# Prompt attention with keys on partitions and rounded products, in a one-core encoder layer

## What is computed

```python
q = (cq @ lp['w_uq']).reshape(B, S, N_HEADS, QK_NOPE + QK_ROPE)
qn, qr = q[..., :QK_NOPE], rope(q[..., QK_NOPE:], pos)
kv = (lat @ lp['w_ukv']).reshape(B, lat.shape[1], N_HEADS, QK_NOPE + V_HEAD)
kn, v = kv[..., :QK_NOPE], kv[..., QK_NOPE:]
sc = mla_scores(qn_b, qr_b, kn, kr)          # 96 features, scaled by 96 ** -0.5
sc = jnp.where(key_chunk[None, :] <= q_chunk[:, None], sc, -jnp.inf)
p = jax.nn.softmax(sc, axis=-1).astype(v.dtype)
return jnp.einsum('bhqk,bkhd->bqhd', p, v)
```

## Time and profile before

| | |
|---|---|
| median of three runs | 1743.34 us |
| profiled execution, its own time | 1737.2 us |
| its span | 1735.4 us |
| mean granted TensorE clock | 0.976 of 2.4 GHz |
| TensorE, VectorE, ScalarE, GpSimd busy | 93%, 57%, 43%, 14% |
| prompt attention, first turned queries to last scaled rows | 323.9 to 525.5 us |
| chain that ended last, TensorE's share | 58% |

### The profile page before, as it was taken

One profiled execution on the slowest core, in us unless ns is written; L12 is line 12 of the kernel. 1 busy time (PEld: TensorE's weight loads), 2 busy tenths in 40 slices (PEclk: granted clock), 3 DMA queues, 4 the chain that ended last, 5 costly groups with the idle time before them and its releaser, 6 DMA issues.

```text
span 1735.4 us, 21728 instructions
## 1 busy us (share of the span) xinstructions
PE 1612.0 (93%) x8282; PEld 1292.7 (74%) x8282; DVE 993.6 (57%) x1347; ACT 751.8 (43%) x1062; POOL 249.4 (14%) x210
## 2 busy tenths in 40 slices
PE   8999999799998899999999998999999999999966
PEld 4578877466766688999877777788888888888852
DVE  1410111366665456422344447889988889889936
ACT  2311111332335202222332113588778778788834
POOL 0000000000007173000021110111111121111104
PEclk9999999999999999999999897999999999999988
DMA  9510111700002354300054445799999999999967
GB/s 356 216 62 29 61 53 47 240 20 20 10 12 98 146 192 172 134 25 13 22 184 149 143 136 216 258 376 379 379 383 387 376 389 385 390 383 377 363 231 299
DMA packets 134295, 351.77 MB, mean 203 GB/s; under 512 B 24498, under 2 KB 27186, under 8 KB 128708
## 3 DMA queue, kind: packets, MB, share of 16 engines
q1 hardware_dynamic: 124084, 330.69, 51.6%
q0 software_dynamic: 9216, 18.89, 2.8%
q10 hardware_dynamic: 912, 1.05, 0.2%
HBM read 322.19 MB, written 43.15 MB: 211 GB/s over the span
## 4 chain that ended last, share of the span: by engine, by line
PE 58%; DMA 20%; DVE 13%; ACT 4%; issue 3%; SPq 1%; POOL 0%; DVEq 0%; POOLq 0%; ACTq 0%
DMA beside<-in_w_exp_up 18%; PE M L911 11%; DVE rounded L1629 10%; PE T L753 6%; PE M L744 5%; PE M L816 3%; PE T L689 3%; PE M L1159 3%; PE T L806 3%; PE M L689 2%; PE T L970 2%; ACT rounded L1517 2%; PE T L972 2%; PE T L971 2%; PE M L999 2%
## 5 line engine op out<-in xcount | busy, mean ns | idle before, releaser
L1159 PE MATMUL M<-rounded 128*128 128x512 f32 x2304 | 548.9, 395 | 11.2 <-DVE conv_w_rows L1960 5.6
L1629 DVE TENSOR_TENSOR rounded<-beside,rounded 128x1024 fp32r<-128x1024 f32 (+2 forms) x394 | 468.0, 1234 | 114.3 <-ACT rounded L1517 56.6
L1159 PEld LDWEIGHTS M<-rounded 128*128 128x128 f32 x2304 | 429.1, 189 | 105.6 <-issue 15.0
L1517 ACT CAST rounded<-beside 128x1024 fp32r<-128x1024 f32 x256 | 259.2, 1050 | 94.9 <-DMA beside<-in_w_exp_up 88.1
L911 PE MATMUL M<-rounded 128*128 128x512 f32 x864 | 216.5, 407 | 5.2 <-DVE logits L1852 2.3
L911 PEld LDWEIGHTS M<-rounded 128*128 128x128 f32 x864 | 164.9, 195 | 43.6 <-issue 7.9
L1527 ACT CAST rounded<-beside 128x1024 fp32r<-128x1024 f32 x128 | 125.3, 1048 | 19.5 <-DMA beside<-in_w_exp_down 17.2
L2201 POOL DMA_INDIRECT expert_rows<-beside,route_out x32 | 44.4, 1389 | 380.1 <-ACT beside L1558 360.6
L1341 ACT ACTIVATE arena<-T,negmax 128x384 f32<-128x384 f32 (+3 forms) x64 | 47.4, 740 | 114.6 <-DVE negmax L1706 114.6
L1629 DVE TENSOR_TENSOR rounded<-T,rounded 128x512 fp32r<-128x512 f32 (+1 forms) x82 | 81.7, 1000 | 26.2 <-ACT rounded L1401 18.2
L689 PE MATMUL T<-tables,arena 128*128 128x128 f32 x572 | 77.8, 284 | 17.3 <-DMA arena<-in_mem_prompt 6.7
(11 more groups left out here) (302 smaller groups left out, 2107.5 us busy)
## 6 DMA issues: line engine op xcount, KB each, us to landing
beside<-in_w_exp_gate SPq DMA_DIRECT2D x64, 1024.0 KB, 8.5
beside<-in_w_exp_up SPq DMA_DIRECT2D x64, 1024.0 KB, 11.3
beside<-in_w_exp_down SPq DMA_DIRECT2D x32, 2048.0 KB, 11.6
arena<-x_rows SPq DMA_DIRECT2D x27, 512.0 KB, 4.0
x_rows<-arena SPq DMA_DIRECT2D x18, 512.0 KB, 3.0
arena<-expert_rows SPq DMA_DIRECT2D x9, 1024.0 KB, 12.8
arena<-in_x_prompt SPq DMA_DIRECT2D x16, 512.0 KB, 3.9
arena<-in_cache_mem_k SPq DMA_DIRECT2D x8, 1024.0 KB, 5.8
```

The source lines that it names most:

```text
L1159: got = nc.tensor.matmul(out, x[xs], (high, low)[ws](w)[:, c:c + 512], start=(first and n == 0), stop=(last and n == 2))
L1517: nc.scalar.copy(high(c), w_raw[c // 4][:, c % 4, :]).then_inc(gu_high, 1)
L1629: return nc.vector.tensor_tensor(out, x, highs.bitcast(f32), ALU.subtract)
```

## The change

Prompt attention is turned: keys stand on partitions, queries along the columns. For each key tile j (0 to 7) `scores` makes the scores of all queries from tile j on, up to 1024 columns, as three rounded products; the masked corners are left out of the exponential and are zeros set once in `p_hi` and `p_lo`. A softmax needs each query's maximum before that. So a first, single rounded product (`lead_scores`, 12 pieces of up to 512 columns in M[0]) gives scores with queries on partitions, VectorE takes their negated maxima (`largest`), and the maximum is written as a 97th feature beside the 96 of each query (`qh[..][:, i, HW:AUG]`), against a row of ones under the keys. The queries are turned again with it (`turn_with_max`), scaled, and split in high and low. ScalarE takes the exponential twice (`exponentials`), to `p_raw` and rounded to `p_hi`; GpSimd subtracts them to `p_lo`. `weigh_values` multiplies 64 value columns beside 64 columns of ones (`v_high`, `v_low`, which stay put) with them, three products, so that M[1] collects result and row sum for each query along the columns; `divide_rows` takes the reciprocal of 64 x 512 sums and multiplies, per half of a head, into `attnT`. The result already has the form in which mixing wants it, so `turn_mix` turns only the conv rows; `conv_rows` has three buffers instead of four.

In the loop over n = 8h + j, TensorE issues scores of n, values of n-2, and for head h+1 lead products (`STEPS`), the second turn, then for head h+2 queries and keys. VectorE's order is keys of h+1, maxima 0 to 2, second half of head h-1's division, maxima 3 to 11, first half of head h's division, low halves of the scaled queries of h+1. w_ukv is loaded after the memory's stores; heads 0 and 1 are loaded before the last tile's stores; w_out's chunks 0 to 3 are loaded after the stage, behind two sets of conv rows.

The core of the diff (of the replaced loops on each engine, which are printed above, only the new side stands here):

```diff
-    ORDER = (2, 4, 6, 7, 5, 3, 1, 0)
+    LEADS = [(i, c, min(c + 512, (i + 1) * 128)) for i in (7, 6, 5, 4, 3, 2, 1, 0) for c in range(0, (i + 1) * 128, 512)]
...
-        conv_rows = [area(at, CW) for at in (46848, 47360, 45312, 45824)]
+        conv_rows = [area(at, CW) for at in (46848, 47360, 45824)]
...
-            sp.wait_ge(mem_ps, 8)
-            sp.dma_start(w_ukv, A["w_ukv"].rearrange("l p (h c) -> p (l h) c", h=H)).then_inc(win_lo_in, 16)
+            sp.wait_ge(mem_out, 48)
+            sp.dma_start(w_ukv, A["w_ukv"].rearrange("l p (h c) -> p (l h) c", h=H)).then_inc(win_lo_in, 16)
...
+            def load_head(h):
+                u = h % 2
+                sp.dma_start(qh[u][:, :, 0:HW], q_heads[:, :, h * HW:(h + 1) * HW]).then_inc(head_in[u], 16)
+                sp.dma_start(wk[u], w_ukv_cols[:, h * (DN + DV):h * (DN + DV) + DN]).then_inc(head_in[u], 16)
+            for u in (0, 1):
+                sp.wait_ge(q_out[u], 16 + 16 * 4)
+            sp.wait_ge(xT_ps, NT)
+            load_head(0)
+            load_head(1)
             store_rows(LAST_TILE)
...
+            sp.dma_start(lat_all, cache_lat).then_inc(cache_in[0], 16)
+            for k in range(4, KT):
                 sp.dma_start(w_out_raw[k], w_out_rows[:, k, :]).then_inc(win_lo_in, 16)
-            sp.dma_start(q_s, q_dram[PT * P:, :].rearrange("p (h c) -> p h c", h=H)).then_inc(sq_in, 16)
-            sp.dma_start(lat_all, cache_lat).then_inc(cache_in[0], 16)
-            sp.dma_start(lat_new[0:ROWS, :, :], lat_s.rearrange("(b r) c -> r b c", r=ROWS)).then_inc(sq_in, 16)
...
-            for t in range(4):
+            load_conv(0)
+            load_conv(1)
+            for k in range(4):
+                sp.dma_start(w_out_raw[k], w_out_rows[:, k, :]).then_inc(win_lo_in, 16)
+            for t in (2, 3):
                 load_conv(t)
...
+            def turn_queries(h):
+                u = h % 2
+                pe.wait_ge(head_in[u], 32 * (h // 2) + 32)
+                for half in (0, 1):
+                    if h > 0:
+                        pe.wait_ge(qa_ready, 2 * (h - 1) + half + 1)
+                    for i in range(4 * half, 4 * half + 4):
+                        got = nc.tensor.transpose(M[0][0:HW, i * P:(i + 1) * P], qh[u][:, i, 0:HW], ident)
+                    got.then_inc(qT_ps, 1)
+            def keys(h):
+                for half in (0, 1):
+                    pe.wait_ge(qT_ready, 2 * h + half + 1)
+                    cols = slice(half * 512, half * 512 + 512)
+                    nc.tensor.matmul(M[0][0:DN, cols], wk[h % 2], latT[:, cols], start=True, stop=True).then_inc(kT_ps, 1)
+            def lead_scores(h, c):
+                i, c0, c1 = LEADS[c]
+                if c < 2:
+                    pe.wait_ge(kT_ready, 2 * h + c + 1)
+                else:
+                    pe.wait_ge(negmax_ready, MAXES * h + c - 1)
+                at = (c % 2) * 512
+                nc.tensor.matmul(M[0][:, at:at + c1 - c0], q_lead[0:HW, i * P:(i + 1) * P], kT_hi[h % 2][0:HW, c0:c1],
+                                 start=True, stop=True).then_inc(lead_ps, 1)
+            def turn_with_max(h):
+                for half in (0, 1):
+                    pe.wait_ge(negmax_ready, MAXES * h + len(LEADS) + half)
+                    for i in range(4 * half, 4 * half + 4):
+                        got = nc.tensor.transpose(M[0][0:AUG, i * P:(i + 1) * P], qh[h % 2][:, i, 0:AUG], ident)
+                    got.then_inc(pT_ps, 1)
+            def by_banks(j):
+                return [(max(c, j * P), c + 512) for c in (0, 512) if j * P < c + 512]
+            def scores(n):
+                h, j = divmod(n, PT)
+                u = h % 2
+                if n > 1:
+                    pe.wait_ge(exp_done, n - 1)
+                if j == 0:
+                    pe.wait_ge(qa_ready, 2 * h + 2)
+                for c0, c1 in by_banks(j):
+                    for m, (k, q) in enumerate(((kT_hi, qa_hi), (kT_hi, qa_lo), (kT_lo, qa_hi))):
+                        got = nc.tensor.matmul(T[n % 2][:, c0:c1], k[u][0:AUG, j * P:(j + 1) * P], q[u][0:AUG, c0:c1],
+                                               start=(m == 0), stop=(m == 2))
+                got.then_inc(s_ps, 1)
+            def weigh_values(n):
+                h, j = divmod(n, PT)
+                at = (h % 2) * DV
+                pe.wait_ge(p_ready, n + 1)
+                if j == 0 and h > 0:
+                    pe.wait_ge(o_done, 2 * h)
+                for c0, c1 in by_banks(j):
+                    for m, (v, p) in enumerate(((v_high, p_hi), (v_high, p_lo), (v_low, p_hi))):
+                        got = nc.tensor.matmul(M[1][:, c0:c1], v[:, j, h // 2, at:at + 2 * DV], p[n % 3][:, c0 - j * P:c1 - j * P],
+                                               start=(j == 0 and m == 0), stop=(m == 2 and j == c1 // P - 1))
+                got.then_inc(o_ps, 1)
...
+            turn_with_max(0)
+            turn_queries(1)
+            keys(1)
+            pe.wait_ge(value_ready, PT)
+            pe.wait_ge(pads_zero, 2)
+            STEPS = ((0, 1, 2), (3, 4, 5), (6, 7), (8, 9), (10, 11))
+            for n in range(PT * H):
+                h, j = divmod(n, PT)
+                scores(n)
+                if n > 1:
+                    weigh_values(n - 2)
+                if h + 1 < H:
+                    if j < 5:
+                        for c in STEPS[j]:
+                            lead_scores(h + 1, c)
+                    if j == 5:
+                        turn_with_max(h + 1)
+                if h + 2 < H:
+                    if j == 6:
+                        turn_queries(h + 2)
+                    if j == 7:
+                        keys(h + 2)
+            weigh_values(PT * H - 2)
+            weigh_values(PT * H - 1)
...
-                if t < PT:
-                    transposes(T[u], attn[:, t, :], 4)
-                transposes(T[u][:, 512:], conv_rows[t % 4], 4).then_inc(rowsT_ps, 1)
+                transposes(T[u][:, 512:], conv_rows[t % 3], 4).then_inc(rowsT_ps, 1)
...
+            def queries_high(h):
+                for half in (0, 1):
+                    cols = slice(half * 512, half * 512 + 512)
+                    act.wait_ge(qT_ps, 2 * h + half + 1)
+                    nc.scalar.copy(q_lead[0:HW, cols], M[0][0:HW, cols]).then_inc(qT_ready, 1)
+            def keys_high(h):
+                for half in (0, 1):
+                    cols = slice(half * 512, half * 512 + 512)
+                    act.wait_ge(kT_ps, 2 * h + half + 1)
+                    if h > 1:
+                        act.wait_ge(s_ps, PT * (h - 1))
+                    nc.scalar.copy(kT_hi[h % 2][0:DN, cols], M[0][0:DN, cols]).then_inc(kT_high, 1)
+            def scaled_high(h):
+                for half in (0, 1):
+                    cols = slice(half * 512, half * 512 + 512)
+                    act.wait_ge(pT_ps, 2 * h + half + 1)
+                    nc.scalar.mul(qa_hi[h % 2][0:AUG, cols], M[0][0:AUG, cols], MLA_SCALE).then_inc(qa_high, 1)
+            def exponentials(n):
+                j = n % PT
+                act.wait_ge(s_ps, n + 1)
+                if n > 1:
+                    act.wait_ge(p_ready, n - 1)
+                if n > 2:
+                    act.wait_ge(o_ps, n - 2)
+                nc.scalar.activation(p_raw[n % 2][:, 0:D - j * P], T[n % 2][:, j * P:], ACT.Exp)
+                nc.scalar.activation(p_hi[n % 3][0:64, 0:64], T[n % 2][0:64, j * P:j * P + 64], ACT.Exp)
+                nc.scalar.activation(p_hi[n % 3][:, 64:D - j * P], T[n % 2][:, j * P + 64:], ACT.Exp).then_inc(exp_done, 1)
...
+            for n in range(PT * H):
+                h, j = divmod(n, PT)
+                exponentials(n)
+                if j == 5 and h + 1 < H:
+                    scaled_high(h + 1)
+                if j == 6 and h + 2 < H:
+                    queries_high(h + 2)
+                if j == 7 and h + 2 < H:
+                    keys_high(h + 2)
...
+            def keys_low(h):
+                for half in (0, 1):
+                    cols = slice(half * 512, half * 512 + 512)
+                    dve.wait_ge(kT_high, 2 * h + half + 1)
+                    take_low(kT_lo[h % 2][0:DN, cols], M[0][0:DN, cols], kT_hi[h % 2][0:DN, cols]).then_inc(kT_ready, 1)
+            def largest(h, c):
+                i, c0, c1 = LEADS[c]
+                at = (c % 2) * 512
+                end = at + c1 - c0
+                dve.wait_ge(lead_ps, len(LEADS) * h + c + 1)
+                if c1 == (i + 1) * P:
+                    nc.vector.memset(M[0][0:64, end - 64:end], FAR).then_inc(dve_step, step.next())
                     dve.wait_ge(dve_step, step.value())
+                into = qh[h % 2][:, i, HW:AUG] if i < 4 else part_max[:, i - 4, c0 // 512:c0 // 512 + 1]
+                nc.vector.tensor_reduce(into, M[0][:, at:end], AX.X, ALU.max, negate=True).then_inc(negmax_ready, 1)
+            def larger_part(h):
```

(39 more changed lines are left out.)

342 lines of the change are left out of this document (154 added, 188 removed).

## The result

The changed kernel takes **1829.1 us** (median of four runs, 1826.5 to 1835.8) against 1741.3 before: a ratio of 1.051, interval 1.0471 to 1.0548. It is slower, as forecast, but by 88 us where 54 were forecast, and 9 above the range. The profiled execution was the slowest of the four, 1835.8 with a span of 1834.0; the other three spans were 1824.6 to 1827.3.

The account below looks back on a forecast made before the run. TensorE, in prompt attention, was taken to bound the kernel. Later cache start 40.2, weights +3.1, mixing -4.1 and clock +14.5 sum to 53.7 us on the median 1743.3: 1797 us, range 1769 to 1820.

Parts of the forecast that it names:

- the mechanism: Prompt attention: each head's two VectorE divisions stand ahead of something TensorE needs; period 29.8 us, 4.8 more than before.
- the two pauses: TensorE idle in each head before the sixth lead product (5.4 us) and before the next queries' transposes (3.7 us).
- The reciprocal: VectorE's reciprocal of 64 x 512 sums takes 4.1 us, from the 1 and 9 column rows; bounds 1.5 and 4.5.
- TensorE's work: Products, transposes and keys of one head in prompt attention sum to 19.3 us against 25.0 before.
- the clock: After the stage's pauses TensorE returns at a granted clock of 0.50, 1.2 GHz; together +14.5 us.
- Pause B: TensorE waits before the next queries' transposes for the first half's division and scaled low half: idle 3.7 us, clock +4.5.
- A: TensorE's lead 5 waits for maximum 3, behind the previous head's division: idle 5.4 us, seven times, clock +10.0.
- Rival 3: Slower still: both pauses leave TensorE at 1.2 GHz for longer, 68 us more in all, 1812; chance 0.2.
- The start: Edge before the first head: maxima end at 338.0, second head's queries and keys take 4 us, scores begin at 342.0.
- three tiles ahead, which is enough: Mixing: a third conv buffer instead of a fourth leaves GpSimd three tiles ahead, taken as enough, at no cost.
- The fallback price: Mixing: if GpSimd's cover were gone, a late conv tile would cost about 9 us, once.
- The weights: Cache part: w_out chunks land 12 us after the stage, and ScalarE's first cache exponential waits for them: +3.1 us.

Follow-up runs that it names:

- experiment 2: The changed kernel with two VectorE steps exchanged, the low half of the scaled queries before the division of a head's first half: 1792.4 us (1.0326).
- experiment 4: The changed kernel with every reciprocal of 64x512 issued twice: 1884.7 us (1.0838).
- experiment 7: The changed kernel with ScalarE copying values and sums out of the accumulator, and VectorE dividing once per pair of heads and half: 1757.1 us (1.011).
- the filled pauses: The changed kernel with 16 and 11 products that nothing reads put into a head's two pauses: 1799.3 us (1.0349).
- experiment 9: The changed kernel with paired divisions, convolutions in the old order, earlier loads, and products that nothing reads at the stage's two edges: 1730.0 us (0.9936).
- experiment 1: The changed kernel with GpSimd's old convolution order in mixing (convolution t+4 behind deviation t), still three buffers: 1810.9 us (1.0429).
- experiment 5: The changed kernel with convolution rows and four w_out chunks issued after the last product instead of the last division: 1829.7 us (1.0524).

## Why the prediction was right and wrong

**Right: the mechanism.** Both divisions lie on TensorE's way, ahead of a maximum and of the low half of the queries; the two pauses appear there, idle 4.4 and 3.1 us. Experiments 2, 4 and 7 show it from three sides: exchange the order, double the cost, take it away. That ScalarE and GpSimd hide beside the heads is right too.

**The reciprocal: 3.36, not 4.1.** It lies within its bounds, near the lower estimate of 3.4 from the 4-column form. The 9-column row pointed too high, by 7.75 ns a column from 1 column and 8.6 from 4. The rule of the Trainium skill that the prediction quoted ("VectorE: DVE Perf Modes", Walkthrough: the 8-slice pipeline in each mode: a repeat of 8 for the divide) gives 4.3 us by an estimate; here the measurement decides, 3.36 us. The shorter reciprocal made the pauses shorter than forecast, idle 8.0 us a head instead of 10.5, and so hid part of the other errors: that the total is no further off is luck to that extent.

**TensorE's work: 20.5, not 19.3.** That is its busy time at full clock in experiment 7. There the keys take 1.93 (1.88 in the sum) and the two turns of queries 2.19 (2.14), so the rest lies in the rounded products; the six scores of the first key tile, for example, need 1.49 us (411.98 to 413.47) where 6 x 0.227 is 1.36. Which of the others cost more than their rows said was not tried.

**The failed step in the stage: the clock.** The sum had 2.1 us a head (+10.0 and +4.5 over seven); the filled pauses show 5.1. Heads were to stand 29.8 apart, 31.9 with the clock; they stand 28.0 apart with the clock held up, 33.1 without. What was wrong is the price of a pause. The kernel before has the shorter stretch behind both gaps that were read: 3.4 us at 0.50, which costs at most 1.7, near the 1.4 and 1.3 in the sum. In the changed kernel eight of the twelve pauses have 6.8 us at 0.50, of which up to 0.7 fall into the pause itself; the rest costs 3.1 to 3.4. Pause B, taken at half of 1.3, has the same two lengths as A. Rival 3 had this mechanism, priced from the same rows at 4.1 a head.

**The start, 4.6 us late.** Up to the twelfth maximum the walk was right within half a microsecond (338.4, forecast 338.0). Then 4 us were put for the second head's queries and keys, and the first head's own turn with the maximum, its scaling and its low halves, 2.7 us (338.4 to 341.1), stand in no term of the sum. The second head's queries and keys took 5.5 us in a stretch at 0.50; at full clock, in experiment 9, they take 3.15 (343.65 to 346.80).

**The failed step outside it: "three tiles ahead, which is enough".** Mixing has 21.5 of the 37 us that the table's rows lie above the sum, more than any other row. With the old order 18.3 of them go (experiment 1); the other 3.2 are for the most part a slower first group (12.8 us there, 11.15 before), and less saved by the transposes than the 4.1. Three buffers were read as the limit, and enough. What counted was GpSimd's order: `deviation(t)` now stands ahead of `convolve(t + 3)`, so the convolution starts 4.3 us after product t ends and takes 9.8, while TensorE has but one more product, 11 us, before it turns that tile. The fallback price, "about 9 us, once", named the right thing, but it recurs, and each wait also makes the next products slow. The range took in neither.

**The weights.** The cache part is 5.0 longer than the sum had it. The weights land 2.3 later than estimated (the issues before them), and the first products run cold, which the sum did not have. In the experiments that keep these loads it takes 66.6 to 72.5 us in one execution each, and with the loads issued earlier (experiment 5) 67.0, so the landing cost nothing that can be told. Filling TensorE's wait behind the last values (experiment 9) did shorten it, by 6 us.

## What to carry to other kernels

When a step is put off by one (t + 3 for t + 4), redo the walk on that engine from what releases it to who needs it; that there are buffers enough says nothing about the order. Price a pause of TensorE with the time that its clock stays down behind it, read as granted clock over the whole stretch and not as the excess of the first instruction. And look first at what stands behind a long instruction on an in-order engine: exchanging two steps gave back 32 to 38 us, with no work removed.

## What the runs showed that was not expected

A wide reciprocal costs 3.36 us for 512 columns on 64 partitions and 3.35 on 128, so stacking two heads on the partitions halves it. After pauses of 2.9 to 4.4 us the granted clock was 0.50 for one of two lengths, 3.4 or 6.8 us, also where the first instruction behind the pause still ran at full clock. 27 products a head that compute nothing made the kernel 30 us faster. The two lengths make a kernel with such pauses scatter: in one execution the two whole heads with both stretches at 6.8 take 33.8 and 34.0 us, the three with one at 3.4 take 32.4 to 32.6, where those of experiment 7 lie between 21.6 and 21.8.
